# A two-block transformer kernel: the order of ScalarE's work within a pair, the first norm's pieces, and the context strip's waits

## The chip, the cores and the metric

The kernel runs on one core of a Trainium2 chip (trn2). The metric is the device time of one execution in microseconds (us). Three runs of the kernel before took 2523.02 to 2527.37 us, median 2526.22.

## What is computed

Two transformer blocks, in float32, on 256 rows of width 2048. The parts that matter here:

```python
def first_block(x, w_in, ..., w_branch, w_out, ln_g, ln_b):
    ...
    out = jnp.einsum('bsd,de->bse', merged, w_out[l])
    x = layer_norm(ALPHA * x + out, ln_g[l], ln_b[l])

def second_block(x, c, ctx, c_ctx, ...):
    mod = (silu_c @ w_ada[l] + b_ada[l])[:, None, :]
    h = rms_norm(x, g_attn[l]) * (1.0 + sc_a) + sh_a
    hc = rms_norm(xc, g_attn[l]) * (1.0 + csc_a) + csh_a
    o_l, o_c = hybrid_mixer(h, hc, w_in[l], w_out[l], ...)
    x = x + gt_a * o_l
    h = rms_norm(x, g_ffn[l]) * (1.0 + sc_f) + sh_f
    x = x + gt_f * swiglu(h, ffn_wg[l], ffn_wu[l], ffn_wd[l])
    return rms_norm(x, g_final)
```

The first block ends with the projection `w_out` and a layer norm over 2048 columns. The second begins with an RMS norm of that result (`h`) and of a context of 256 rows (`hc`); both are multiplied with the same `w_in`. Between the two norms and the feed-forward part lie four kinds of attention with their softmaxes.

## The kernel before, in words

**Weights.** Every large product is float32 made of three matmuls in a faster format. A weight tile is split in a high half `whi`, rounded by ScalarE (`hi`, L882 to 889, recorded at the helper's line L880), and the rest `wlo`, by VectorE (`lo`, L1259 to 1266, row line L1264). The row side (activations) is kept as a high and a low half too: `xh`/`xl`, `mh`/`ml`, `hch`/`hcl` and so on. `sub` (PE, L2010 to 2033) multiplies high by high, high by low and low by high.

**Strips and pairs.** The program is a list of strips (a strip is up to 512 weight columns), each cut in pairs of two 128-row weight tiles. The pairs, numbered through the whole program, are the clock of the order: every engine has a loop over this number, called the beat (`until(b)` holds a piece of side work back until beat b). In beat i TensorE does pair i and then its side work. ScalarE in beat i empties finished accumulators (`evacuate`), then goes once round all its side chains (L1242, 1243), and last makes the high half of pair i + 4 (L1244, 1245). That high half waits for the landed weights and for the end of pair i - 1 on TensorE, since five split buffers are used in turn. VectorE in beat i evacuates, does its side chains, then the low half of pair i + 4, and then its share of the products with `w_ada` (`ada`, L1268 to 1288, recorded at L1283 and L1286). Most strips serve 256 rows (two row blocks `tb`, 12 matmuls a pair); those that serve `ALL` four row blocks take twice as long.

**Queues.** All weights are loaded by SyncE's queue into six raw buffers (L602 to 630), a load of `w_ada` among them from time to time; each waits until VectorE has used what lay in the buffer. GpSimd does the powers of -1/2 of the norms (`power`, L641) and small loads; ScalarE issues one store of `x1` (L1070).

**Around the end of the first block.** While the four `wo` strips run (8 pairs each; wo3 ends at beat W), the context is normalised block by block (`scaled_T` on PE, `hT` on VectorE L1583 to 1605, `hT_high` on ScalarE L1038 to 1048): TensorE transposes and scales two 128-column pieces, VectorE writes them to `sg` (L1596), ScalarE makes their high half (`hch`), and VectorE in the next beat the low half (`hcl`, L1603). This is done for eight row pairs of each of two blocks; the second block ends in beat W - 2. Strip nkc, the first of the second block, begins in beat W + 1, and TensorE waits at its start for the last low half (`ktneed`, L403). From beat W + 1 VectorE evacuates wo3, aggregates the statistics and does the layer norm on `x1` (`norm1`, L1640 to 1660): two instructions of 2048 columns for each row block, in beats W + 2 and W + 4. ScalarE squares each block (L1068), GpSimd takes the powers (L773 to 775), VectorE makes the scaled diagonals (L1611), and in beats W + 10 to W + 18 the result is transposed as the context was (`hx`, L1665).

**Elsewhere.** `heads1` (ScalarE L1010 to 1036), `attend` (L1081), `diff` (L1135), `ot_high` (L1164) and `norm2` (L1171) are side chains of ScalarE. In `ot_high` and `norm2` VectorE needs ScalarE's result in the same beat (L1769, L1894).

Of the kernel before, what the change touches and what calls it, by code (L numbers as in the profile page):

```python
# [117 lines left out]
def flat(ap):  # L118
    return ap.rearrange("p a b -> p (a b)")
# [14 lines left out]
def program(nc, I, out):  # L134
    ctx = ExitStack()
    with ctx:
        sems = {}

        def S(name):
            if name not in sems:  # L140
                sems[name] = ctx.enter_context(nc.semaphore(name))
            return sems[name]
# [256 lines left out]
        def win2(name, c0, n, tbs, evac, ktneed=None):  # L399
            strip(name, W2[:, c0:c0 + n], range(16), n, st2, tbs, evac, ktneed=ktneed)  # L400

        CTN = (("hcT", 1, 7), ("sq1", 1))
        win2("nkc", 512, 512, CT, ("copy", lambda tb: flat(na_k[:, tb, :, :]), CTN), lambda kt, tb: ("hcl", 1, 7))  # L403
        win2("nvc", 1024, 512, CT, ("copy", lambda tb: na_v[:, tb, :], ()))
        win2("nq", 0, 512, XT, ("copy", lambda tb: flat(na_q[:, tb, :, :]), (("hxT", 7),)),
             lambda kt, tb: ("hxl", kt // 2))
# [226 lines left out]
        def pool(eng, dry):  # L633
# [3 lines left out]
            def until(b):  # L637
                while beat[0] < b:
                    yield
# [129 lines left out]
            def norm1():  # L769
                yield from until(B["x1"])  # L770
                for tb in range(2):
                    power(rs[:, 2 + tb:3 + tb], 1, "ln1", tb)
                yield from until(B["x1"] + 5)  # L773
                for tb in range(2):
                    power(rs[:, 6 + tb:7 + tb], 1, "rms1", tb)

# [93 lines left out]
        def act(eng, dry):  # L870
# [4 lines left out]
            def until(b):  # L875
                while beat[0] < b:
                    yield
# [13 lines left out]
            def evacuate(s, tb):  # L891
                kind, n, ps = s.evac[0], s.ncols, main_ps(s, tb)
                if kind == "copy":
                    W.wait_ge("acc", s.name, tb)
                    for key in s.evac[2]:
                        W.wait_ge(*key)
                    copy(s.evac[1](tb), ps).then_inc(*M.inc(S("evac_act"), "ea", s.name, tb))
                elif kind == "kv":
                    W.wait_ge("acc", s.name, tb)
                    W.wait_ge("yT", "B", 3)  # L900
                    k = ps[:, 0:128].rearrange("p (k d) -> p k d", k=2)
                    copy(kd[:, tb, :, 0, :], k)
                    copy(kd[:, tb, :, 1, :], k)
                    copy(vv[:, tb, :], ps[:, 128:256]).then_inc(*M.inc(S("evac_act"), "ea", s.name, tb))
                elif kind in ("silu", "glu", "silumul", "gate"):
                    W.wait_ge("acc", s.name, tb)
                    if tb in sg_free:
                        W.wait_ge(*sg_free[tb])
                    else:
                        W.wait_ge("par")  # L910
                    eng.activation(sg[:, tb, 0:n], ps, ACT.Sigmoid).then_inc(*M.inc(S("evac_act"), "ea", s.name, tb))
                    sg_free[tb] = ("ev", s.name, tb)
                    if kind == "gate":
                        sg_free[tb] = ("ev", "b" + s.name[1:], tb)
                elif kind == "ffg":
                    W.wait_ge("acc", s.name, tb)
                    k = s.evac[1]
                    if k == 0:
                        W.wait_ge("h2T", 1, 3)
                    elif k == 6:  # L920
                        W.wait_ge("ev", "wd03", tb)
                    else:
                        W.wait_ge("ev", f"fu{k - 1}", tb)
                    eng.activation(sil[:, tb, :], ps, ACT.Sigmoid).then_inc(*M.inc(S("evac_act"), "ea", s.name, tb))
                elif kind == "out2":
                    k = s.evac[1]
                    W.wait_ge("ev", s.name, tb)
                    if k:
                        W.wait_ge("sq2", k - 1, tb)
                    else:  # L930
                        W.wait_ge("pv", "ml", 3)
                    eng.activation(sqj[:, tb, :], x2[:, tb, k * 512:(k + 1) * 512], ACT.Square,
                                   accum_out=smx[:, 0, 0, 4 * tb + k:4 * tb + k + 1]) \
                        .then_inc(*M.inc(S("squares"), "sq2", k, tb))
                elif kind == "down" and s.evac[1] == 1:
                    k = s.evac[2]
                    W.wait_ge("ev", s.name, tb)
                    if k:
                        W.wait_ge("sq3", k - 1, tb)
                    else:  # L940
                        W.wait_ge("h2l", 1, 3)
                    eng.activation(gfx[:, tb, 0:512], x2[:, tb, k * 512:(k + 1) * 512], ACT.Square,
                                   accum_out=smx[:, 1, 0, 4 * tb + k:4 * tb + k + 1]) \
                        .then_inc(*M.inc(S("squares"), "sq3", k, tb))
# [116 lines left out]
            def norm1():  # L1061
                yield from until(B["x1"])
                yield from until(B["x1"] + 2)
                for tb in range(2):
                    yield from until(B["x1"] + 2 + 2 * tb)
                    W.wait_ge("x1", tb)
                    W.wait_ge(*(("sq1", 0) if tb else ("csq", 1)))
                    eng.activation(sqt[:, :], x1[:, tb, :], ACT.Square, accum_out=rs[:, 4 + tb:5 + tb]) \  # L1068
                        .then_inc(*M.inc(S("squares"), "sq1", tb))
                eng.dma_start(scr_x1, x1[:, :, :]).then_inc(*M.inc(S("scr_x1"), "scr_x1", by=16))  # L1070
                yield from hT_high("hx", B["hx"], hxh, ((), 0, 256), ("acc", "wo3", 1))
# [158 lines left out]
            for i in range(NSUB + 2):  # L1230
                beat[0] = i
                if i + 4 < 8:
                    xT(i + 4)
                for s in strips:
                    if s.end == i and len(s.tbs) == 4:
                        for tb in s.tbs[:3]:
                            evacuate(s, tb)
                    for tb in s.tbs[3:] if len(s.tbs) == 4 else s.tbs:
                        late = s.evac[0] in ("out2", "down") and s.evac[-1] < 3
                        if closed[s.name, tb] == i - 1 - late:  # L1240
                            evacuate(s, tb)
                for g in chains:  # L1242
                    next(g, None)
                for j in split_at.get(i, ()):  # L1244
                    hi(j)

        def dve(eng, dry):
# [5 lines left out]
            def until(b):  # L1255
                while beat[0] < b:
                    yield
# [382 lines left out]
            def norm1():  # L1640
                yield from until(B["x1"])
                for tb in range(2):
                    W.wait_ge("stz", 3, tb)
                    eng.bn_aggr(mvz[:, tb, :], flat(stz[:, tb, :, :])).then_inc(*M.inc(S("ln_dve"), "mvz", tb))
                    W.wait_ge("mvz", tb)
                    ts(rs[:, 2 + tb:3 + tb], mvz[:, tb, 1:2], 1.0, EPS_LN, ALU.mult, ALU.add) \
                        .then_inc(*M.inc(S("var"), "var", "ln1", tb))
                W.wait_ge("lnr", 1)
                for tb in range(2):
                    yield from until(B["x1"] + 1 + 2 * tb)  # L1650
                    x = x1[:, tb, :]
                    W.wait_ge("rstd", "ln1", tb)
                    stt(x, x, mvz[:, tb, 0:1], lnr[0][:, :], ALU.subtract, ALU.mult).then_inc(*M.inc(S("x1"), "x1a", tb))  # L1653
                    W.wait_ge("x1a", tb)
                    stt(x, x, rs[:, 2 + tb:3 + tb], lnr[1][:, :], ALU.mult, ALU.add).then_inc(*M.inc(S("x1"), "x1", tb))  # L1655
                yield from until(B["x1"] + 5)
                for tb in range(2):
                    W.wait_ge("sq1", tb)
                    variance(rs[:, 4 + tb:5 + tb], 1, 2048, EPS_RMS, rs[:, 6 + tb:7 + tb], "rms1", tb)
                yield from until(B["x1"] + 6)  # L1660
                W.wait_ge("hcT", 1, 7)
                for tb in range(2):
                    W.wait_ge("rstd", "rms1", tb)
                    diagonal(dgx[:, tb, :], rs[:, 6 + tb:7 + tb], "rms1", tb)
                yield from hT("hx", B["hx"], acx[:, 0, :], mod[:, 0, :], hxh, hxl,  # L1665
                              ((), 0, 256), ("hcl", 1, 7), ("hcl", 1, 6))
# [781 lines left out]
```

## Time and profile before

| | |
|---|---|
| runs | 2523.02, 2526.22, 2527.37 us |
| profiled execution | 2528.11 us, its span 2526.4 us |
| TensorE busy | 98% of the span (11467 matmuls) |
| VectorE busy | 71% |
| ScalarE busy | 43% |
| mean granted TensorE clock | 0.992 |

The profile is one execution. In its timeline a row gives start, duration, engine, line, operation, out<-in and, in brackets, how long the engine stood idle before it and what ended that. Matmuls overlap by design (one takes some 0.39 us and the next starts 0.23 us after it), so a busy TensorE is read from the absence of idle time.

### The profile page before, as it was taken

The page shows a single profiled execution, that of the slowest core. Times are in us where ns is not written, and L with a number is a line of the kernel's source. Part 1 is how long each engine was busy: PE and PEld are TensorE (multiplying, and loading weights), DVE is VectorE, ACT ScalarE, POOL GpSimd, SP SyncE. Part 2 cuts the span into 40 slices and gives each one's busy share as a digit, 9 for nine tenths or more (in the row PEclk, how much of TensorE's full clock was granted, in tenths as well). Part 3 has the DMA queues.
Part 4 walks back from the last instruction along what each step waited for, and adds up shares of the span by engine and source line. Part 5 has one row for each costly group of instructions (what it writes and reads, how often), then busy time and mean ns, then how long its engine had stood idle before and what let it go on. Part 6 is the DMA issues. An engine that isn't in the chain of part 4 may idle for free.

```text
span 2526.4 us, 29299 instructions
## 1 busy us (share of the span) xinstructions
PE 2472.3 (98%) x11467; PEld 2033.5 (80%) x11467; DVE 1785.3 (71%) x2429; ACT 1083.4 (43%) x1405; POOL 92.2 (4%) x131
## 2 busy tenths in 40 slices
PE   8999999999999999998999999899999999999998
PEld 6888888888888888887787888667788888888886
DVE  5678868888897877778778757466877655555555
ACT  4334444444354554433443333554444443444443
POOL 2000000000000000000011100000000000000000
PEclk9999999999999999999999999999999999999999
DMA  8868766666687668876796656246688766666663
GB/s 293 272 205 272 245 215 194 195 186 194 207 256 249 200 200 287 291 233 208 234 304 203 200 183 223 86 142 208 216 256 264 236 208 194 192 191 185 191 191 125
DMA packets 276023, 545.42 MB, mean 216 GB/s; under 512 B 18247, under 2 KB 23021, under 8 KB 274476
## 3 DMA queue, kind: packets, MB, share of 16 engines
q1 hardware_dynamic: 268768, 514.91, 64.7%
q0 software_dynamic: 6128, 26.34, 3.3%
q10 hardware_dynamic: 988, 2.29, 0.3%
q8 instruction: 90, 1.47, 0.2%
q14 instruction: 49, 0.40, 0.1%
HBM read 534.15 MB, written 9.32 MB: 215 GB/s over the span
## 4 chain that ended last, share of the span: by engine, by line
PE 89%; DVE 5%; issue 3%; ACT 2%; DMA 0%; ACTq 0%; POOL 0%; POOLq 0%; DVEq 0%
PE pb L2004 87%; PE pb L2008 2%; ACT whi L880 1%; DVE acc L1286 1%; DVE wlo L1264 1%; DVE sg L1596 1%; DMA raw<-in_w_in 0%; ACT pb L1020 0%; DVE sg L1888 0%; DVE x L1655 0%; DVE x L1653 0%; DVE d_o L1511 0%; DVE x L1341 0%; DVE sm L1822 0%; ACTq L948 0%
## 5 line engine op out<-in xcount | busy, mean ns | idle before, releaser
L1264 DVE TENSOR_TENSOR wlo<-raw,whi 128x1024 fp32r<-128x1024 f32 x790 | 953.1, 1212 | 545.0 <-ACT whi L880 542.8
L880 ACT ACTIVATE whi<-raw 128x1024 fp32r<-128x1024 f32 x790 | 826.0, 1049 | 928.0 <-PE pb L2004 854.8
L2004 PE MATMUL pb<-whi,xh 128*128 128x512 f32 (+1 forms) x1184 | 467.1, 394 | 7.0 <-DVE wlo L1264 7.0
L2004 PE MATMUL pb<-whi,xl 128*128 128x512 f32 (+1 forms) x1184 | 459.4, 388 | 0.0
L2004 PE MATMUL pb<-wlo,xh 128*128 128x512 f32 (+1 forms) x1184 | 459.0, 388 | 0.0
L1286 DVE SCALAR_TENSOR_TENSOR acc<-raw,silc,acc 128x512 f32<-128x512 f32 x480 | 344.0, 747 | 6.5 <-DMA raw<-in_w_ada 1.4
L2004 PE MATMUL pb<-whi,fh 128*128 128x512 f32 x704 | 277.2, 394 | 3.9 <-DVE fl L1895 3.9
L2004 PE MATMUL pb<-whi,fl 128*128 128x512 f32 x704 | 274.8, 390 | 0.0
L2004 PE MATMUL pb<-wlo,fh 128*128 128x512 f32 x704 | 274.5, 390 | 0.0
L2004 PEld LDWEIGHTS pb<-whi,xh 128*128 128x128 f32 x1184 | 223.3, 189 | 54.7 <-DVE wlo L1264 9.1
L2004 PEld LDWEIGHTS pb<-whi,xl 128*128 128x128 f32 x1184 | 223.2, 189 | 46.2
L2004 PEld LDWEIGHTS pb<-wlo,xh 128*128 128x128 f32 x1184 | 223.6, 189 | 43.4
L2004 PE MATMUL pb<-whi,mh 128*128 128x512 f32 (+1 forms) x448 | 181.5, 405 | 6.5 <-DVE wlo L1264 6.5
L2004 PE MATMUL pb<-whi,ml 128*128 128x512 f32 (+1 forms) x448 | 173.3, 387 | 0.0
L2004 PE MATMUL pb<-wlo,mh 128*128 128x512 f32 (+1 forms) x448 | 173.0, 386 | 0.0
L2004 PEld LDWEIGHTS pb<-whi,fh 128*128 128x128 f32 x704 | 132.6, 188 | 31.1 <-issue 3.3
L2004 PEld LDWEIGHTS pb<-whi,fl 128*128 128x128 f32 x704 | 132.5, 188 | 28.1
L2004 PEld LDWEIGHTS pb<-wlo,fh 128*128 128x128 f32 x704 | 132.7, 188 | 27.0
L2004 PE MATMUL pb<-whi,idh 128*128 128x512 f32 x352 | 137.3, 390 | 0.0
L2004 PE MATMUL pb<-whi,idl 128*128 128x512 f32 x352 | 137.0, 389 | 0.0
L2004 PE MATMUL pb<-wlo,idh 128*128 128x512 f32 x352 | 137.0, 389 | 0.0
L2004 PEld LDWEIGHTS pb<-whi,mh 128*128 128x128 f32 x448 | 84.8, 189 | 25.5 <-DVE wlo L1264 8.7
(412 smaller groups left out, 2851.1 us busy)
## 6 DMA issues: line engine op xcount, KB each, us to landing
raw<-in_w_in SPq DMA_DIRECT2D x376, 512.0 KB, 4.5
raw<-in_w_ada SPq DMA_DIRECT2D x192, 512.0 KB, 4.7
raw<-in_ffn_wg SPq DMA_DIRECT2D x88, 512.0 KB, 4.4
raw<-in_ffn_wu SPq DMA_DIRECT2D x88, 512.0 KB, 4.3
raw<-in_ffn_wd SPq DMA_DIRECT2D x88, 512.0 KB, 3.9
raw<-in_w_branch SPq DMA_DIRECT2D x64, 512.0 KB, 4.1
raw<-in_w_out SPq DMA_DIRECT2D x64, 512.0 KB, 4.5
scr_band<-bandt POOLq DMA_DIRECT2D x2, 1536.0 KB, 8.6
```

Source lines behind the costliest of these rows:

```text
L880: return eng.activation(dst, src, ACT.Copy)
L1264: ins = tt(wlo[:, u, 0:d, 0:n], raw[:, l % NRAW, 0:d, 0:n], f32(whi[:, u, 0:d, 0:n]), ALU.subtract)
L1286: ins = stt(a, raw[:, l % NRAW, k, :], c, a, ALU.mult, ALU.add)
L1596: ins = ts(sg[:, kp % 2, k * n:(k + 1) * n], side(key + "T", *w[0], kp)[:, k * n:(k + 1) * n], Ac[:, kt:kt + 1], Bc[:, kt:kt + 1], ALU.mul ...
L2004: return eng.matmul(dst, l, r, start=start, stop=stop)
L2008: return eng.transpose(dst, src, ident[0:n, 0:n])
```

## The change

ScalarE's loop over the pairs makes the high halves before it goes round its side chains (they came after). The two norm instructions of each row block become four of 1024 columns, so that the norm is spread over four beats, W + 2 to W + 5, and not done in two; the squares, the powers and the diagonals are allowed one beat later. TensorE's wait at the start of strip nkc is for the low half of the row pair that the matmul reads, not for the last one.

```diff
-        win2("nkc", 512, 512, CT, ("copy", lambda tb: flat(na_k[:, tb, :, :]), CTN), lambda kt, tb: ("hcl", 1, 7))
+        win2("nkc", 512, 512, CT, ("copy", lambda tb: flat(na_k[:, tb, :, :]), CTN), lambda kt, tb: ("hcl", 1, kt // 2))
...
@@ GpSimd, norm1 @@
-                yield from until(B["x1"] + 5)
+                yield from until(B["x1"] + 6)
...
@@ ScalarE, norm1 @@
-                    yield from until(B["x1"] + 2 + 2 * tb)
+                    yield from until(B["x1"] + 3 + 2 * tb)
...
@@ ScalarE, the loop over the pairs @@
+                for j in split_at.get(i, ()):
+                    hi(j)
                 for g in chains:
                     next(g, None)
-                for j in split_at.get(i, ()):
-                    hi(j)
...
@@ VectorE, norm1 @@
                 for tb in range(2):
-                    yield from until(B["x1"] + 1 + 2 * tb)
-                    x = x1[:, tb, :]
                     W.wait_ge("rstd", "ln1", tb)
-                    stt(x, x, mvz[:, tb, 0:1], lnr[0][:, :], ALU.subtract, ALU.mult).then_inc(*M.inc(S("x1"), "x1a", tb))
-                    W.wait_ge("x1a", tb)
-                    stt(x, x, rs[:, 2 + tb:3 + tb], lnr[1][:, :], ALU.mult, ALU.add).then_inc(*M.inc(S("x1"), "x1", tb))
-                yield from until(B["x1"] + 5)
+                    for c in range(2):
+                        yield from until(B["x1"] + 1 + 2 * tb + c)
+                        cs = slice(c * 1024, (c + 1) * 1024)
+                        x = x1[:, tb, cs]
+                        stt(x, x, mvz[:, tb, 0:1], lnr[0][:, cs], ALU.subtract, ALU.mult) \
+                            .then_inc(*M.inc(S("x1"), "x1a", tb, c))
+                        W.wait_ge("x1a", tb, c)
+                        stt(x, x, rs[:, 2 + tb:3 + tb], lnr[1][:, cs], ALU.mult, ALU.add) \
+                            .then_inc(*M.inc(S("x1"), "x1c", tb, c))
+                    M.value["x1", tb] = M.value["x1c", tb, 1]
+                yield from until(B["x1"] + 6)
...
-                yield from until(B["x1"] + 6)
+                yield from until(B["x1"] + 7)
```

## Rows read from the trace of the kernel before

**Rows 1.** The page's busy times; one pair in the chain that ended last.

```profile
PE 2472.3 (98%) x11467; PEld 2033.5 (80%) x11467; DVE 1785.3 (71%) x2429; ACT 1083.4 (43%) x1405; POOL 92.2 (4%) x131
...
2232.15 2.76 PE pb L2004 x12
```

**Rows 2.** Waits, whole span: us in total, times, longest.

```profile
PE pb L2004 <- DVE wlo L1264: 17.4, 10, 2.8
...
ACT whi L880 <- PE pb L2004: 854.8, 505, 6.4
```

**Rows 3.** Waits of TensorE, 1107 to 1260 us, same columns.

```profile
PE pb L2004 <- DVE wlo L1264: 10.4, 6, 2.8
PE pb L2004 <- issue: 2.8, 1, 2.8
```

**Rows 4.** Stretches: us, busy PE, PEld, DVE, ACT, POOL, clock, DMA share, GB/s.

```profile
1107.00:1140.00 33.00, 33.00 (x162) 27.59 (x161) 24.43 (x43) 10.61 (x16) 0.58 (x1) 1.00 0.70 223
1140.00:1150.00 10.00, 7.18 (x26) 5.85 (x26) 7.83 (x12) 6.12 (x7) 1.10 (x2) 0.66 0.65 196
...
1180.00:1223.00 43.00, 36.25 (x161) 29.11 (x161) 37.66 (x45) 17.89 (x21) 4.36 (x5) 0.96 0.76 259
1223.00:1260.00 37.00, 33.30 (x168) 27.24 (x167) 28.59 (x41) 15.60 (x21) 0.00 (x0) 1.00 0.65 195
```

**Rows 5.** Waits of VectorE and ScalarE, 1107 to 1260 us, same columns.

```profile
DVE wlo L1264 <- ACT whi L880: 29.1, 28, 1.9
...
ACT hch L880 <- DVE sg L1596: 47.2, 16, 4.6
ACT mh L880 <- DVE sg L1596: 21.4, 8, 3.6
```

**Rows 6.** Timeline of VectorE and ScalarE in one beat of the context's norm.

```profile
1124.22 0.73 DVE L1596 TENSOR_SCALAR sg<-pb,acx,mod 128x128 f32<-128x128 f32 x2
...
1124.98 0.42 ACT L880 ACTIVATE hch<-sg 128x256 fp32r<-128x256 f32 x1 [3.39 <-DVE sg L1596]
1125.31 1.04 ACT L880 ACTIVATE whi<-raw 128x1024 fp32r<-128x1024 f32 x1
...
1126.38 1.23 DVE L1264 TENSOR_TENSOR wlo<-raw,whi 128x1024 fp32r<-128x1024 f32 x1 [1.10 <-ACT whi L880]
```

**Rows 7.** Timeline of ScalarE and TensorE where TensorE first stands still there.

```profile
1141.18 3.88 ACT L880 ACTIVATE whi<-raw 128x1024 fp32r<-128x1024 f32 x4
...
1143.53 0.80 PE L2004 MATMUL pb<-whi,mh 128*128 128x512 f32 x1 [2.82 <-DVE wlo L1264]
```

**Rows 8.** Timeline of VectorE at the end of wo3 and in the first norm.

```profile
1181.85 0.99 DVE L1603 TENSOR_TENSOR hcl<-sg,hch 128x256 fp32r<-128x256 f32 x2
...
1189.67 0.68 DVE L1341 SCALAR_TENSOR_TENSOR x<-x,pb 128x512 f32<-128x512 f32 x1
...
1194.18 2.34 DVE L1653 SCALAR_TENSOR_TENSOR x<-x,mvz,lnr 128x2048 f32<-128x2048 f32 x1
1196.56 2.35 DVE L1655 SCALAR_TENSOR_TENSOR x<-x,rs,lnr 128x2048 f32<-128x2048 f32 x1
...
1215.72 0.28 DVE L1611 TENSOR_SCALAR dgx<-ident,rs 128x128 f32<-128x128 f32 x1 [0.23 <-POOL rs L643]
```

**Rows 9.** The page, costliest groups: count, busy us, mean ns, idle before.

```profile
L1286 DVE SCALAR_TENSOR_TENSOR acc<-raw,silc,acc 128x512 f32<-128x512 f32 x480 | 344.0, 747 | 6.5 <-DMA raw<-in_w_ada 1.4
```

**Rows 10.** Timeline of TensorE at four stops outside that stretch.

```profile
1346.31 0.50 PE L2004 MATMUL pb<-whi,hch 128*128 128x512 f32 x1 [1.11 <-ACT gq_q L880]
...
806.68 0.88 PE L2008 MATMUL pb<-ident,pb 128*128 128x128 f32 x6 [0.28 <-ACT smx L1023]
...
1464.35 1.09 PE L2008 MATMUL pb<-ident,ppb 128*128 128x128 f32 x8 [1.26 <-ACT pp L1088]
...
1777.63 0.77 PE L2004 MATMUL pb<-whi,fh 128*128 128x512 f32 x1 [3.15 <-DVE fl L1895]
```

**Rows 11.** Stretch of the differential attention, columns of rows 4.

```profile
1603.00:1660.00 57.00, 49.25 (x219) 35.63 (x220) 34.15 (x74) 29.86 (x70) 3.24 (x6) 0.85 0.36 111
```

## The prediction

> **What bounds the kernel now.** I began with the page: TensorE is busy for 98% of the span [rows 1], so only what makes TensorE stand still, or run slowly, is worth anything; a pair of 12 matmuls takes 2.76 us when nothing is in the way [rows 1]. The waits of the whole span come next: TensorE's largest one is for VectorE's low halves, 17.4 us in 10 stops [rows 2]. Asked for 1107 to 1260 us alone, the same view gives 10.4 us of these in 6 stops, and 2.8 us put down to "issue" [rows 3]. That stop is at the start of strip nkc: VectorE's last low half of the context ends at 1182.84 [rows 8], just before the strip starts, and L403 waits for exactly that. So 13.2 us of standing still lie in 150 us around the end of the first block. The view by stretches adds that the granted clock is 0.66 over 1140 to 1150 and 0.96 over 1180 to 1223, against 1.00 before and after [rows 4]: of its two levels, 1.2 and 2.4 GHz, it falls to the lower for (1 - 0.66) x 2 x 10 = 6.8 us and (1 - 0.96) x 2 x 43 = 3.4 us, each time at a stop of 2.8 us.
>
> Why is VectorE late? In that stretch it stood waiting 28 times, 29.1 us, for ScalarE's high halves of weights, and ScalarE itself stood 68.6 us waiting for `sg` [rows 5]. One beat shows the knot: VectorE writes `sg`, ScalarE waits 3.39 us for it, makes `hch` and only then the weights' high half (1.04 us), and VectorE, with nothing else to do, waits 1.10 us for that [rows 6]. ScalarE had the time to make it earlier. The end of this is seen at 1141.18: four high halves in a row without any wait between them, so all were ready, and TensorE stands until the first of them has its low half [rows 7].
>
> **The change part by part.** First the order on ScalarE. In most pairs it alters nothing, since the high half waits for TensorE's previous pair anyway (854.8 us of such waits [rows 2]) and TensorE needs it some three pairs later. Where ScalarE waits for `sg`, the high half now fills that wait, and VectorE gets back about 1.05 us a beat. In the context's norm VectorE had 24.43 busy us in 33 [rows 4], and the 29.1 us of waits [rows 5] lie for the most part in three series of eight row pairs (two of the context, one of `hx`), so about one of 1.1 us in each beat; without them its work fits beside TensorE's, it stays less than a beat or two behind, and both the stops in the wo strips and the one at nkc lose their cause, as do the three small ones at 1250 to 1260. Of the 13.2 us I take all as removable. The lower clock goes with the stops. TensorE works at it for 2.0 to 3.4 us worth in the first case (6.8 us, with or without the stop in it, halved; I take 2.7) and at most 1.7 in the second (I take 1.5): 4.2 us. Together 17.4.
>
> Second the norm in smaller pieces. Between the end of wo3 and the first transposes of `hx` TensorE has ten pairs, 27 to 28 us with the small products between them. VectorE took from 1189.67, its first evacuation, to 1216.00, the last diagonal, which is 26.3 us, 3 of them waits [rows 8]. It started 6.8 us after the context's last low half [rows 8] because it was behind; now it starts nearly at once when wo3 ends. So this chain just fits. The small pieces see to it that no low half is kept waiting for more than 2.6 us by the norm (4.7 before), but eight instructions cost more than four: 0.747 us for 512 columns [rows 9] and 2.34 for 2048 [rows 8] give about 1.28 for 1024, 0.22 more for each pair, 0.9 us of VectorE in all. The bounds are nothing and a full 0.747 for each of the four added, 3.0 us. I leave 1.5 us of standing still here for this chain and for weight loads that come late. The trace shows two instructions of 2048 in a row with 0.04 us between them; the Trainium skill (VectorE: DVE Perf Modes, the section on the TRN2 errata) speaks against such a cut: every instruction with SBUF operands pays a fixed extra cost, 151 cycles at 0.96 GHz in its fp32 formula. By that, an estimate, the cut costs 4 x 0.16 = 0.6 us of VectorE instead of 0.9, and the sum is 0.3 us better at most. Squares, powers and diagonals move one beat later, with their one ScalarE store and GpSimd's queue behind them (one `b_ada` load); I cost that at nothing, since ScalarE and GpSimd have room [rows 4]. If VectorE were a beat behind, the diagonals would come late instead, which is the second rival.
>
> Third the context wait pair by pair. Alone it would save at most the 2.8 us and their clock; with VectorE no longer behind, the last low half is done nearly three pairs before nkc begins, and the finer wait is worth nothing more. I count it within the 17.4.
>
> Then what the new order costs. Where ScalarE's side work is what TensorE waits for and the high half used to come behind it, it is now 1.04 us later [rows 6]. The trace has such places: the exponentials of the first four heads, for which TensorE waits 0.28 us at 806.68; the first block of `gq` softmaxes at 1464.35 (1.26 us); and `norm2`, where VectorE needs ScalarE's high half in the same beat, at 1777.63 (3.15 us) [rows 10]. I take 1.0, 1.0 and, because part of the two high halves there fits in ScalarE's idle time, 0.7 and another 0.6 two beats later: 3.3 us. At 1346.31 the high half stood between the exponentials and the evacuation for which TensorE waits 1.11 us, and it now goes ahead of the exponentials' own wait: 1.0 gained. In the differential attention (1603 to 1660, where TensorE stands for 57 - 49.25 = 7.8 us and the clock is 0.85 [rows 11]) some high halves now delay `ot_high` by half a microsecond, and others free VectorE sooner; I take 0, with 3 us either way.
>
> **The sum.** -17.4 + 1.5 - 1.0 + 3.3 = -13.6 us. The profiled execution took 2528.11 us around its span of 2526.4, 1.9 over the median; on it the result would be 2514.5, on the median of the runs 2526.22 - 13.6 = 2512.6. A measurement of this kernel tells about 0.2%, 5 us, from no change.
>
> **The rivals.** (1) As forecast, more or less: TensorE's stops between 1107 and 1260 go, and small ones come elsewhere. 2507 to 2517 us. For it: rows 6 and 7 show the cause directly. Chance 0.60, and 0.05 for still better, 2502 to 2507, if VectorE's gained time also mends the softmax stretch.
>
> (2) The chain of the norm takes the place of the low halves. It fits with a microsecond or two to spare; if VectorE still comes a beat late to wo3's end, TensorE waits for the diagonals at beat W + 10 by about 3 us and falls to its lower clock for another 1.7, and loads come late behind it: -13.6 + 3 + 1.7 + 1 gives about 2518.5. Against it: 29.1 us of VectorE's waits are gone by then. Chance 0.15.
>
> (3) No change that can be measured, 2521 to 2531. The high half waits for landed weights as well, and the raw buffers come free only with VectorE's low halves; if the loads are what comes late, the side work of a beat now waits behind a load, and VectorE behind the side work. Then half of 13.2 stays, the clock with it, and the 3.3 us of costs remain: -6.6 + 3.3, about 2523. Against it: no wait for a load stands in the beats of rows 6 and 7. Chance 0.12.
>
> (4) Slower. The place is the softmax chains between 1320 and 1740 us: twenty blocks of exponentials, each now behind a high half. If TensorE has no slack there, each costs it 1.04 us, 20.8 in all, and the stretch of rows 11 runs longer at the lower clock, say 5 us more. With the gain kept at 16 that is +10, 2536 us. It decides where the slack between the exponentials and TensorE's transposes is under 1 us in more than 12 of the 20; rows 10 show two such places. Chance 0.08. That the change doesn't do what it says could only hold for the third part, see above.
>
> Of TensorE's clock the Trainium skill (TensorE: Matmul & The Clock Gate, Part 1) says that the throttled rate is the default and activity releases it. The trace agrees in that the clock fell at both 2.8 us stops of the stretch. By that rule the added microsecond at 1464.35 could cost a spell at the lower clock too, some 1.7 us by rows 4; the sum goes without it.
>
> **How the numbers follow.** Predicted 2512.6, the likeliest case. Its own range is 2507 to 2517. Rivals 1 and 2 with the better case hold 0.80; the range goes from 2504 to 2521. Faster than 2521.2: 0.60 + 0.05 + 0.15 = 0.80; within 5 us 0.12; slower 0.08.
>
> **What would show it.** Right: from 1107 to 1260 TensorE's waits fall from 13.2 to under 3 us, VectorE's waits for `whi` there from 29.1 to under 8, the clock reads 1.00 throughout; ScalarE's high half stands ahead of `hch` in each beat; VectorE's first evacuation of wo3 comes within 2 us of TensorE's start of nkc; the stops at 806, 1464 and 1777 have grown by about 1 us each. Wrong: new waits of TensorE for `dgx` or `hxl`, ScalarE's waits for raw loads grown from a few microseconds to tens, or a longer stop in the stretch of rows 11 that gives back more than 5 us.

## The result and the profile after

| | before | after |
|---|---|---|
| median of 6 runs each | 2527.03 us (2523.02 to 2528.24) | 2510.27 us (2508.52 to 2510.84) |
| ratio, 95% interval | | 0.9934 (0.9922 to 0.9947) |
| profiled execution, its span | 2528.11, 2526.4 us | 2510.84, 2509.1 us |

Faster by 0.66%, where 2512.6 us was forecast. The profiled execution of after is 0.6 us over its median.

The page of after, TensorE's busy time and the low halves, which answers to [rows 1]. Line numbers of TensorE have moved by 5, those of VectorE's and ScalarE's split have not:

```profile
PE 2466.2 (98%) x11467; PEld 2032.2 (81%) x11467; DVE 1781.8 (71%) x2433; ACT 1088.2 (43%) x1405; POOL 95.2 (4%) x131
...
L1264 DVE TENSOR_TENSOR wlo<-raw,whi 128x1024 fp32r<-128x1024 f32 x790 | 952.4, 1212 | 460.7 <-ACT whi L880 458.0
```

The four instructions more on VectorE are the cut of the norm. Its waits for high halves are 458.0 us over the whole span, 542.8 before.

The waits of after over the whole span (us, times, longest), against the 17.4 us in 10 stops and the 854.8 us of [rows 2]:

```profile
ACT whi L880 <- PE pb L2009: 1090.0, 621, 6.9
...
PE pb L2009 <- DVE wlo L1264: 8.2, 4, 2.9
```

ScalarE now waits far longer for TensorE with its high halves (1090.0 us): it comes to them sooner, and TensorE has only then to let a buffer go. Around the end of the first block that wait costs nothing: TensorE does not stand still there.

The waits of after between 1107 and 1260 us, against [rows 3] and [rows 5]:

```profile
ACT hch L880 <- DVE sg L1596: 17.8, 16, 3.4
ACT mh L880 <- DVE sg L1596: 10.8, 8, 2.5
...
DVE wlo L1264 <- ACT whi L880: 6.1, 5, 2.2
```

No row of TensorE's matmuls waiting for `wlo` is left, nor the one called "issue". VectorE's 29.1 us have become 6.1.

The stretches of after, columns as in [rows 4]. The first four have the times of the rows before:

```profile
1107.00:1140.00 33.00, 33.00 (x163) 27.85 (x162) 26.95 (x47) 14.65 (x19) 1.13 (x2) 1.00 0.76 253
1140.00:1150.00 10.00, 10.00 (x54) 8.52 (x53) 9.46 (x14) 4.56 (x6) 1.45 (x2) 1.00 0.73 239
1180.00:1223.00 43.00, 42.98 (x213) 35.89 (x212) 39.91 (x53) 19.29 (x22) 3.86 (x5) 1.00 0.84 286
1223.00:1260.00 37.00, 37.00 (x181) 31.19 (x180) 31.73 (x42) 18.79 (x23) 0.54 (x1) 1.00 0.86 278
...
1440.00:1455.00 15.00, 12.80 (x63) 11.02 (x63) 6.63 (x12) 8.04 (x18) 0.00 (x0) 0.89 0.56 180
...
1756.00:1768.00 12.00, 8.90 (x30) 7.20 (x31) 9.62 (x23) 4.01 (x6) 1.46 (x1) 0.72 0.32 103
```

TensorE is busy all the time around the end of the first block, and its clock is 1.00 there. The last two rows are places where it still stands and slows down.

The timeline of TensorE in after, its stops outside that stretch, against [rows 10]:

```profile
34.99 0.51 PE L2009 MATMUL pb<-whi,xh 128*128 128x512 f32 x1 [1.39 <-DVE wlo L1264]
...
809.19 0.88 PE L2013 MATMUL pb<-ident,pb 128*128 128x128 f32 x6 [1.23 <-ACT smx L1023]
...
879.28 0.88 PE L2013 MATMUL pb<-ident,pb 128*128 128x128 f32 x6 [0.81 <-ACT smx L1023]
...
1446.14 1.09 PE L2013 MATMUL pb<-ident,ppb 128*128 128x128 f32 x8 [2.20 <-ACT pp L1088]
...
1759.10 0.77 PE L2009 MATMUL pb<-whi,fh 128*128 128x512 f32 x1 [3.72 <-DVE fl L1900]
```

806, 1464 and 1777 of before have grown by 0.95, 0.94 and 0.57 us of idle time; the stop of [rows 10] at 1346 is gone; 34.99 was 0.45 us and 879.28 nothing.

The timeline of after, one beat of the context's norm, the counterpart of [rows 6], and the end of that norm:

```profile
1108.41 1.06 ACT L880 ACTIVATE whi<-raw 128x1024 fp32r<-128x1024 f32 x1 [1.66 <-PE pb L2009]
...
1110.29 0.73 DVE L1596 TENSOR_SCALAR sg<-pb,acx,mod 128x128 f32<-128x128 f32 x2
...
1110.93 1.22 DVE L1264 TENSOR_TENSOR wlo<-raw,whi 128x1024 fp32r<-128x1024 f32 x1
1111.06 0.42 ACT L880 ACTIVATE hch<-sg 128x256 fp32r<-128x256 f32 x1 [1.58 <-DVE sg L1596]
...
1171.28 0.43 DVE L1603 TENSOR_TENSOR hcl<-sg,hch 128x256 fp32r<-128x256 f32 x1 [0.15 <-ACT hch L880]
...
1176.31 0.39 PE L2009 MATMUL pb<-whi,hch 128*128 128x512 f32 x1
...
1177.92 0.68 DVE L1341 SCALAR_TENSOR_TENSOR x<-x,pb 128x512 f32<-128x512 f32 x1
...
1182.88 1.28 DVE L1655 SCALAR_TENSOR_TENSOR x<-x,mvz,lnr 128x1024 f32<-128x1024 f32 x1
```

The high half is made before ScalarE's wait for `sg`, so VectorE goes from `sg` straight to the low half. The context's last low half is done at 1171.71, 4.6 us before strip nkc starts, and the first evacuation of wo3 comes 1.6 us after that start. The last row is the first of the cut instructions.

**Where the 17.3 us went.** The start of the same matmul in the two profiled executions was compared at marks along the span, and the growth of the difference (after less before) put down to the stretch between two marks:

| stretch (time before) | after less before, us |
|---|---|
| start, to 50 us | +1.6 |
| 806, heads' exponentials | +0.95 |
| 852, spell at the lower clock absent | -1.4 |
| 879, heads' exponentials | +1.0 |
| 1106 to 1262 | -19.7 |
| 1346 | -1.4 |
| 1464, `gq` | +2.3 |
| 1600 to 1660, differential attention | -2.5 |
| 1777, norm2 | +1.85 |
| sum | -17.3 |

### The profile page after: what moved, and what is told of

The parts are those of the page before. It is cut to its first block, busy times and chain, and to the rows that moved or that the text cites. A ratio compares the mean times of both kernels' runs of the same rounds, so it can differ in the third digit from the quotient of the medians.

```text
span 2509.1 us, 29311 instructions
## 1 busy us (share of the span) xinstructions
PE 2466.2 (98%) x11467; PEld 2032.2 (81%) x11467; DVE 1781.8 (71%) x2433; ACT 1088.2 (43%) x1405; POOL 95.2 (4%) x131
## 4 chain that ended last, share of the span: by engine, by line
PE 95%; DVE 2%; ACT 2%; issue 1%; ACTq 0%; POOL 0%; POOLq 0%; DVEq 0%
PE pb L2009 92%; PE pb L2013 2%; DVE acc L1286 1%; DVE wlo L1264 0%; ACT whi L880 0%; ACT pb L1020 0%; DVE d_o L1511 0%; ACTq L948 0%; DVE sm L1827 0%; DVE sg L1333 0%; ACT L1020 0%; DVE sg L1893 0%; DVE d_o L1517 0%; ACTq L952 0%; ACT ppb L1142 0%
## 5 line engine op out<-in xcount | busy, mean ns | idle before, releaser
L880 ACT ACTIVATE whi<-raw 128x1024 fp32r<-128x1024 f32 x790 | 828.4, 1051 | 1170.2 <-PE pb L2009 1090.0
L1264 DVE TENSOR_TENSOR wlo<-raw,whi 128x1024 fp32r<-128x1024 f32 x790 | 952.4, 1212 | 460.7 <-ACT whi L880 458.0
L1511 DVE SCALAR_TENSOR_TENSOR d_o<-glT,cw,d_o 128x256 f32<-128x256 f32 x240 | 104.0, 480 | 0.0
```

Of the source, the lines that this page charges most:

```text
L880: return eng.activation(dst, src, ACT.Copy)
L1264: ins = tt(wlo[:, u, 0:d, 0:n], raw[:, l % NRAW, 0:d, 0:n], f32(whi[:, u, 0:d, 0:n]), ALU.subtract)
L1511: ins = stt(d, glT[:, f, k:k + 256], w, d, ALU.mult, ALU.add)
```

## The experiments

The theory of the prediction is that the order on ScalarE alone makes the gain. The rival is that the smaller pieces of the norm and the finer wait carry a part of it. Three kernels do one part of the change each.

**The order alone.** On the kernel before:

```diff
+                for j in split_at.get(i, ()):
+                    hi(j)
                 for g in chains:
                     next(g, None)
-                for j in split_at.get(i, ()):
-                    hi(j)
```

> The kernel before with ScalarE's high halves ahead of its side chains, and nothing else of the change. Theory 1 (the order carries the gain: VectorE is late because the high half waits behind side work that waits for sg): 15.5 to 17.5 us faster than before, as the whole change, with no stop of TensorE for a low half between 1107 and 1245 us; the norm's 2048-column instructions delay a low half by 4.7 us, but VectorE is no longer behind and has that much in hand. Theory 2 (the smaller pieces and the finer wait carry their part): at most 12 us faster, with stops at the start of nkc (2.8 us) and in the norm (1.7 and 2.2 us) left.

2508.74 us (2505.17 to 2511.05), ratio 0.9926 (0.9911 to 0.9941). Its waits between 1107 and 1260 us:

```profile
PE pb L2004 <- DVE wlo L1264: 0.5, 1, 0.5
```

The whole gain is here: 18.5 us between the medians, where theory 1 had 15.5 to 17.5 and theory 2 at most 12. Between 1106 and 1262 us it is ahead of before by 19.4 us, against 19.7 for the full change, and at every place from 806 us on it steps as in the table. One stop of 0.5 us at 1195.89, where theory 1 had none, is all that the other two parts take away.

**The pieces alone**, with the old order and the old wait:

```diff
-                    yield from until(B["x1"] + 1 + 2 * tb)
+                    for c in range(2):
+                        yield from until(B["x1"] + 1 + 2 * tb + c)
+                        cs = slice(c * 1024, (c + 1) * 1024)
...
-                yield from until(B["x1"] + 5)
+                yield from until(B["x1"] + 6)
```

> The kernel before with the norm in 1024-column pieces and the later squares, powers and diagonals, and nothing else. Theory 1: VectorE itself is what is late from 1183 to 1260, and smaller pieces only let other low halves come first; what TensorE does not lose at 1200 and 1209 it loses by 1260. Within 1 us of before. Theory 2: the stops of 1.7 and 2.2 us go, 3 to 4 us faster.

2525.46 us (2524.89 to 2528.17), ratio 0.9997 (0.9988 to 1.0007): no change. Its waits in the stretch:

```profile
DVE wlo L1264 <- ACT whi L880: 27.8, 26, 1.7
...
PE pb L2009 <- DVE wlo L1264: 6.7, 4, 2.8
PE pb L2009 <- issue: 2.7, 1, 2.7
```

The pieces do take stops away (10.4 us of waits for `wlo` became 6.7: two stops in nkc became one of 1.26 us at 1203.60), yet by 1262 us only 0.4 us of that was left, since the clock fell there. VectorE's waits stay at 27.8: the cause is untouched.

**The fine wait alone:**

```diff
-        ... lambda kt, tb: ("hcl", 1, 7))
+        ... lambda kt, tb: ("hcl", 1, kt // 2))
```

> The kernel before with the context strip's wait row pair by row pair, and nothing else. Theory 1: strip nkc starts about 1.6 us earlier, but the low half that TensorE waits for at 1200 comes when VectorE makes it, so that stop grows by as much; within 1 us of before, unless the spell at the lower clock goes too (1.6 us). Theory 2: 2.8 us of standing and 1.6 us of the lower clock go, 3 to 4.5 us faster.

2527.97 us (2524.47 to 2528.77), ratio 1.0001 (0.9992 to 1.001). Waits in the stretch, then TensorE's timeline:

```profile
PE pb L2004 <- DVE wlo L1264: 12.8, 9, 2.8
```

```profile
1193.73 0.50 PE L2004 MATMUL pb<-whi,hch 128*128 128x512 f32 x1 [1.22 <-DVE wlo L1264]
...
1199.51 0.80 PE L2004 MATMUL pb<-whi,hch 128*128 128x512 f32 x1 [2.75 <-DVE wlo L1264]
```

This is a wait that only moves: between 1106 and 1262 us this profile gains 0.1 us on that of before. The 2.8 us called "issue" at the start of nkc are gone, and the waits for low halves grew by 2.4 in their place: VectorE's backlog is the same, and TensorE meets it over the next six pairs.

**A smaller dose of the order**, ahead only while the context's first series of norm pieces runs:

```diff
+                first = B["hc"][0] <= i < B["hc"][1]
+                for j in split_at.get(i, ()) if first else ():
+                    hi(j)
                 for g in chains:
                     next(g, None)
-                for j in split_at.get(i, ()):
+                for j in split_at.get(i, ()) if not first else ():
                     hi(j)
```

> The kernel before with the high halves ahead only in the twelve beats of the context's first row block (beats of its square up to that of the second one's). Theory 1: the stop at 1143 (2.8 us) and the lower clock behind it go, 4 to 5.6 us faster; VectorE's waits for high halves from 1107 to 1140 fall from about 8 us to under 2; the stops at nkc, 1200, 1209 and 1250 to 1260 stay as they are, since the second block's eight beats put VectorE behind by themselves. Against it: if the lateness is one long accumulation, the stops behind shrink too and more than 8 us are gained; if it does not come from the order, nothing is.

2523.28 us (2520.35 to 2525.19), ratio 0.9986 (0.9977 to 0.9996). That is 3.9 us between the medians, just under the 4 to 5.6 forecast. In its profile the stop of [rows 7] and the lower clock behind it are gone, 5.8 us gained by 1150. Then 1.6 are lost up to the start of nkc: TensorE meets VectorE's backlog in two new stops of 0.26 and 0.29 us, and the stop at nkc is 3.3 us instead of 2.8. By 1262 us 3.6 are left. The stops at 1200 and 1209 are as before. VectorE's waits for high halves between 1107 and 1140 us are 0.8 us instead of 8.0, and 21.1 instead of 29.1 up to 1260. So the gain follows the beats in which the order is changed.

**Which of the places outside pay.** Two kernels kept the whole change, but chose the beats of the new order (same form of edit as the last one, with another `first`):

```diff
+                first = B["hc"][0] <= i <= B["hx"][7] + 2
```

> Order ahead only in the beats from the start of the context's norm to the end of hx's; pieces and fine wait as in the changed kernel. If the gain is made in that stretch and the rest of the program pays and gets back small sums: from 1107 to 1262 us the same 19.7 us less than before; the high half's cost at the start (1.0), at 806 (0.95), at 879 (1.0), at 1446 (1.0 and a spell at the lower clock, 1.6) and in norm2 (1.85) are gone, but so are the gains at 852 (1.4), at 1346 (1.4) and in the differential attention (2.5 net). Together 2527.2 - 19.7 = 2507.5 us. Rival: the order outside the stretch is a net gain, because VectorE keeps its lead; then this one stands above the changed kernel, at 2512 or more.

2506.59 us (2505.86 to 2507.99), ratio 0.9922 (0.9908 to 0.9936). The forecast of 2507.5 holds and the rival's 2512 falls: outside the stretch the new order is a small net loss. In its profile the steps at 806, 879 and 1464 are 0.0, 0.0 and 0.5 us. Not all parts came as listed: norm2 still costs 1.35 us there, the differential attention still gains 1.4, and the first 50 us are 0.9 shorter than before's.

```diff
+            behind = {B["heads"][0] + 3, B["heads"][2] + 3, *range(9), *range(B["h2"][0] + 1, B["h2"][1] + 3)}
+            behind |= {B["gq"][h] + 1 for h in range(4)} | set(B["ot"])
...
+                first = i not in behind
```

> The changed kernel with the high half behind the side work again at the places where it was seen to cost: the first nine beats, two of the heads' exponentials, the beat of each gq exponential, the ot_high beats, norm2. If each cost is just the 1.04 us of a high half that stands ahead of what TensorE waits for: 1.0 + 0.95 + 1.0 + (1.0 + 1.6) + 1.85 = 7.4 us less than the changed kernel's 2510.3, so 2503 us, with the differential attention open by 1.5 us either way. Rival: behind the side work the high half makes VectorE late in the same places, and what is saved comes back as stops for wlo: 2508 to 2511.

2502.86 us (2501.65 to 2503.46), ratio 0.9905 (0.989 to 0.992): better than both kernels, and as forecast. But the parts are not all as forecast. Against after, the start (+0.3 instead of +1.6), 806 (0), 879 (0) and 1464 (-0.3 instead of +2.3) gave 5.8 us; the spell at 852 came back (1.6 lost); norm2 gave 0.5 instead of 1.85; and the differential attention 2.6 more than in after. The sum holds in part because misses cancel.

**The clock at 1464.** The prediction left a lower clock there out of its sum. Two kernels put the high half behind the side work in one single beat of the changed kernel:

```diff
+                first = i != B["gq"][0] + 1
```

> The changed kernel with the high half behind the exponentials in one single beat, that of the first gq block. TensorE's stop at 1446 falls from 2.2 to about 1.2 us. Theory A, the stop's length decides on the clock: the spell at the lower clock at 1447.5 goes with it, and by 1460 us the kernel is 1.0 + 1.6 = 2.6 us ahead of the changed one, 2507.7 in all. Theory B, the spell comes by itself or by any stop there: the clock still falls at 1446, and only 1.0 us is saved, 2509.3.

2509.41 us (2508.9 to 2511.32), ratio 0.9934 (0.9921 to 0.9946). This was the wrong beat. The high half moved behind the exponentials at 1417, where nobody waits, and the stop at 1446 stayed. The stop belongs to the third block:

```diff
+                first = i != B["gq"][2] + 1
```

> The same test as the last one, with the third gq block instead of the first: the high half stands behind the exponentials in that one beat, and its 1.05 us are what TensorE waits for at 1446. The stop falls from 2.2 to about 1.2 us. Theory A (the stop's length decides on the clock): no spell at the lower clock at 1447.5, 2.6 us in all, 2507.7. Theory B: the clock falls there all the same, 1.0 us, 2509.3.

2507.03 us (2506.49 to 2508.01), ratio 0.9922 (0.991 to 0.9935). Its timeline of TensorE at that stop, then the row for the stretch, columns as in [rows 4]:

```profile
1444.64 1.09 PE L2016 MATMUL pb<-ident,ppb 128*128 128x128 f32 x8 [1.26 <-ACT pp L1088]
```

```profile
1440.00:1455.00 15.00, 13.74 (x71) 11.25 (x70) 7.14 (x11) 8.89 (x19) 0.00 (x0) 1.00 0.51 165
```

One high half of 1.05 us, moved behind two exponentials: the stop is 0.94 us shorter, and the granted clock over these 15 us is 1.00 instead of 0.89. That is 2.6 us up to 1480, the step of +2.3 turned into -0.3. The medians are 3.2 us apart, the two profiles 4.35; of the rest in the profiles 1.1 lies in the differential attention and 0.3 at the start. All twelve profiles agree on this place: the three with a stop of 2.20 or 2.21 us (after, the order alone, the wrong beat) have the lower clock behind it, the nine with 1.26 us do not.

**The spell at 852.** It stands in the kernel before and in the chosen order, and not in the changed kernel. Here the chosen order, with one beat changed back:

```diff
-            behind = {B["heads"][0] + 3, B["heads"][2] + 3, ...
+            behind = {B["heads"][2] + 3, ...
```

> The chosen order, 2502.86 us, but with the high half ahead of the exponentials again in one beat, that of the first four heads. TensorE's stop at 806 comes back at 1.2 us (+0.95). Theory A: the spell at the lower clock at 853, 44 us later, is tied to that stop: with the stop it is absent, as in the changed kernel, -1.4, so 0.45 us less in sum. Theory B: the spell has to do with other parts of the order, and it stays: +0.95 us.

2502.86 us (2502.74 to 2503.02), ratio 0.9906 (0.9892 to 0.9919). The stretch where the spell lies:

```profile
848.00:858.00 10.00, 10.00 (x52) 8.67 (x52) 4.82 (x12) 1.63 (x3) 0.50 (x1) 0.83 0.40 113
```

The stop at 806 is back (+1.0 in the profile) and the spell stays, so theory A falls. TensorE is busy for 10.00 of 10 us there and the clock is 0.83 all the same. The median did not rise by 1.0; in the differential attention this profile gained 1.5 us more than that of the chosen order on the same code, which hides the cost in it. The kernel with the fine wait alone shows the spell absent without any change in the code. Up to 1170 us it issues what before does, and the row for its stretch reads

```profile
848.00:858.00 10.00, 10.00 (x59) 8.76 (x58) 6.53 (x13) 2.76 (x3) 0.50 (x1) 1.00 0.49 144
```

So this spell comes and goes on the same code. Whether the change has a share in its absence is open. Of the twelve profiles it is absent in five: the four with the new order in the first beats (after, the order alone, the two of the clock at 1464) and that of the fine wait. These five are 0.56 to 1.56 us later than before at 50 us; the seven that have the spell are at most 0.30 later. Why a late start should matter at 852 no run shows, but the new order's 0.94 us at the start (see below) would bring most kernels over that line.

**The chosen order without the other two parts**, on the kernel before:

> The chosen order on the kernel before, without the norm's smaller pieces and the finer wait. If these two are worth nothing: 2502 to 2504 us, as with them (1 to 2 us less were possible, since the order alone came out 1.5 us under the changed kernel). Rival: with the other stops gone they begin to matter, and without them the kernel is slower by the 1 to 3 us of a stop in the norm of x1: 2504 to 2506.

2501.85 us (2501.23 to 2502.82), ratio 0.9901 (0.9886 to 0.9917), the fastest of all. Even where nothing else stands in the way, pieces and fine wait give nothing.

## Why the prediction was right

**The cause, and the order as the cure: shown.** The order alone gives the full gain, a part of its beats gives that part of the gain, and the other two parts give none. VectorE's waits for high halves fell to 6.1 us (under 8 was forecast), and the signs in the profile came as written: `whi` ahead of `hch`, clock 1.00, first evacuation within 2 us.

**The size of it was too small, -15.9 against -19.7.** The 13.2 us of stops went, all of them. The term "+1.5 left for the norm chain and late loads" was not needed: no matmul of TensorE waits for `dgx` or a weight in the stretch. The lower clock was sized right: matmul by matmul, the two spells of before cost 2.7 and 1.7 us, where 2.7 and 1.5 were taken. The seven stops were sized too small by their idle time. From start to start of the matmuls they cost 14.3 us, 1.1 more than 13.2. This is the overlap that idle time leaves out: it counts from a matmul's end, 0.39 us after its start, and the next one would have started after 0.23, which is 0.16 us for each stop. Of the 1.0 us that is left, 0.5 is the second matmul behind five of the stops, which starts 0.34 us after the first and not 0.23; the last 0.5 us are not accounted for.

**The pieces and their price.** 1.28 us for 1024 columns was the forecast, and 1.28 is what the timeline of after has (1182.88). The price hides beside TensorE. The rule on fixed cost drawn from the Trainium skill (VectorE: DVE Perf Modes, the section on the TRN2 errata) gave 0.16 us for each instruction added (that section has it for `tensor_tensor`, and this is another operation); the two rows give 2 x 1.28 - 2.34 = 0.22, so the measured one decides. Of the worth of this part the prediction said too much: the pieces were to "see to it that no low half is kept waiting for more than 2.6 us by the norm", and with the order changed the whole instructions cost one stop of 0.5 us.

**The fine wait: right.** "Worth nothing more" once VectorE is in time; alone it saved nothing, since the wait moved. The last low half was done 4.6 us ahead of nkc, though, less than two pairs and not the nearly three of the prediction.

**The costs of the order.** At 806, +0.95 (1.0 forecast). At 1346, -1.4 (-1.0). At 1464 the idle time grew by the forecast microsecond, 1.26 to 2.20, and then the clock fell, which the sum left out: +2.3 instead of 1.0. (It is the third block of `gq`, not the first as the prediction has it.) Here the aside on the Trainium skill (TensorE: Matmul & The Clock Gate, Part 1), that throttled is the default, would have been the better guide. The prediction priced the spell that it allowed for at 1.7 us, by [rows 4], and 1.6 came. In norm2 the stop grew by 0.57 us (3.15 to 3.72) where 1.3 was forecast, and it did so in every kernel with the new order there. The other 1.3 of the measured 1.85 are not the order's: the chosen order has the old one there and the short stop, and its step was +1.35 and +1.39 in two kernels with the pieces and +0.2 without, where the granted clock over 12 us is 0.86, not 0.72:

```profile
1749.00:1761.00 12.00, 9.34 (x44) 7.92 (x45) 10.80 (x28) 4.42 (x6) 1.55 (x1) 0.86 0.34 112
```

The pieces alone had no spell at this place at all and gained 1.5 us by 1781, so they are not its cause: this is scatter of the spell's length.

**What was not forecast.** Two places: 879, the heads' second such beat, where a stop of 0.81 us appeared that before did not show at all, and the start of the program, where the stop at 34.99 is 1.39 us. There the high half stands ahead of ScalarE's sigmoid and exponential (L962, L964), and TensorE waits for a low half that VectorE makes only behind its use of their results: 0.94 us more than in before, in all four kernels with this order. The other 0.6 us of the step come before 18 us, while the first inputs and weights land. I had looked for places where TensorE already waited for ScalarE's side work. A place where it was in time by less than 1.04 us pays as well, and those show no stop. Over all the kernels run, the first 50 us vary by -0.9 to +0.9 us against before with the old order there, and by +0.6 to +1.6 with the new.

**The differential attention**: 0 with 3 either way, measured -2.5. Between 1560 and 1660 us the four kernels with the old order throughout that stretch stand at -1.2 to -1.4, so the profile of before was 1.2 us on the slow side there; the four with the new order at -2.5 to -3.6; the three with the chosen one at -4.7 to -6.6. The new order thus seems worth some 1 to 2 us in this stretch, and more when the high half stays behind the side work where `ot_high` is made, which is the delay that the prediction had guessed. With so few profiles and a scatter of 2 us among those three on equal code, these sizes are rough.

**The rivals.** The norm chain late: it is not, 1.28 us pieces or 2.34. No change by late loads: ScalarE's waits for landed weights in the stretch are 8.4 and 6.2 us, where they were 8.5 and 3.8, and they hold up nothing on TensorE. Slower by the softmax chains: of the twenty blocks one pays (1464), with two of the first attention's; that was the right place to look at, and the slack is there. The eight rows of the table outside 1106 to 1262 sum to +2.4 us, and without the -1.4 at 852 and the 0.6 of the start to +3.2. The prediction had +2.3 for them. That the two agree is luck: the start, 852 and 879 stood in no term, 1464, norm2 and the differential attention were off by 0.5 to 2.5 us, and the misses cancel.

## What to carry to other kernels

When a consumer waits for an engine that itself waits for the consumer's output, put the work that is ready ahead of the wait; look at the waits of each engine for the other, not at TensorE's stops, which come 30 us later. The reverse also holds: where the bound engine waits for the side work, a microsecond ahead of it is a microsecond lost, and so is it where the slack is smaller than that microsecond; the order is best chosen beat by beat (2501.85 against 2508.74 us here). Finer pieces and finer waits treat the backlog, not its cause: alone each moved the stop or gave it back.

## What was unexpected of the hardware

A stop's price is not its idle time. The stop of 2.20 us at 1446 brought the lower clock and the one of 1.26 us in the same place did not: 0.94 us of idle cost 2.6. But the length alone doesn't tell. In the kernel before, the stops at 1209.00 and 1255.75, both of 2.21 us, left the clock at 1.00. The second of them, of the same length and at the same matmul, brought the lower clock in the kernel with the smaller dose. TensorE's timeline of before and of that kernel, then the stretch of each:

```profile
1255.75 0.50 PE L2004 MATMUL pb<-whi,mh 128*128 128x512 f32 x1 [2.21 <-DVE wlo L1264]
...
1251.44 0.67 PE L2007 MATMUL pb<-whi,mh 128*128 128x512 f32 x1 [2.21 <-DVE wlo L1267]
```

```profile
1255.00:1260.00 5.00, 3.49 (x14) 2.60 (x15) 4.64 (x7) 3.36 (x4) 0.00 (x0) 1.00 0.49 159
...
1250.00:1260.00 10.00, 8.56 (x31) 6.92 (x32) 9.41 (x12) 5.62 (x7) 0.00 (x0) 0.83 0.65 190
```

And at 852 the clock fell with TensorE busy throughout. The same code gave spells of different length, or none, at 852, behind the stop at 1143 (0.66 over 1140 to 1150 in before; the fine wait's profile lost 1.0 us less there), in norm2 and in the differential attention, worth 1 to 2 us each, which is the floor for what one profiled execution can tell of a place like these.
